# A two-layer decoder trunk on one core: the pair loop of TensorE on a fixed slot of the program, waits moved to their use, two k-tiles moved, two PSUM slots swapped

## The reference

```
h = rms_norm(x, norm_g);  z = h @ w_in      # columns of z feed all that follows
y_rnn = (rg_lru(x_rnn) * silu(g_rnn)) @ rg_out
y_sc  = (sc_b * conv3(sc_c * x_sc) * silu(g_sc)) @ sc_out
q = rms_norm(rms_norm(c_q) @ w_uq);  k = rms_norm([rms_norm(c_kv) @ w_uk, k_rope]);  v = rms_norm(c_kv) @ w_uv
y_att = (causal_attention(rope(q), rope(k), v) * silu(g_att)) @ mla_out     # 8 heads
x = x + (sig(g0) * y_rnn + sig(g1) * y_sc + sig(g2) * y_att) @ w_out
```

## Time and profile before

| | before |
|---|---|
| median of 3 runs | 1804.34 us (1803.9 to 1805.08) |
| profiled execution: own time / span | 1801.34 / 1799.5 us |
| mean granted clock of TensorE | 0.991 |
| busy: PE, PEld | 1742.7 us (97%), 1634.6 us (91%) |
| busy: POOL, DVE, ACT | 1184.6 us (66%), 807.1 us (45%), 469.6 us (26%) |
| chain that ended last | PE 95% |

### The profile page before, as it was taken

How to read it: one execution, slowest core, us unless ns; L and a number is a source line. 1 busy time by engine, 2 the same in 40 slices (tenths; PEclk the granted TensorE clock), 3 DMA queues, 4 the chain that set the end, 5 groups by cost and what they waited for, 6 DMA issues and landing times.

```text
span 1799.5 us, 32868 instructions
## 1 busy us (share of the span) xinstructions
PE 1742.7 (97%) x12264; PEld 1634.6 (91%) x12264; DVE 807.1 (45%) x1373; ACT 469.6 (26%) x843; POOL 1184.6 (66%) x1365
## 2 busy tenths in 40 slices
PE   3998998989999999999999999999999999999999
PEld 3998998989999999999999899999998888888887
DVE  3764554436464453212246645555556544522121
ACT  3422323222233223101124323232322333311110
POOL 6474644536677886777775747465557888877773
PEclk9999999999999999999999999999999999999999
DMA  3322221212222323222342212212122222332233
GB/s 126 136 71 65 71 81 43 93 54 71 83 83 93 105 82 119 93 94 83 122 152 74 93 64 70 80 64 80 54 86 91 91 93 93 105 128 95 94 118 107
DMA packets 47515, 162.03 MB, mean 90 GB/s; under 512 B 5408, under 2 KB 6816, under 8 KB 47136
## 3 DMA queue, kind: packets, MB, share of 16 engines
q1 hardware_dynamic: 41328, 146.56, 25.0%
q10 hardware_dynamic: 6112, 14.39, 2.2%
HBM read 152.27 MB, written 10.81 MB: 91 GB/s over the span
## 4 chain that ended last, share of the span: by engine, by line
PE 95%; issue 1%; POOL 1%; DVE 1%; ACT 1%; DMA 0%; ACTq 0%; POOLq 0%; DVEq 0%
PE slots L507 83%; PE slots L565 4%; PE slots L598 2%; PE slots L657 2%; PE slots L541 2%; PE slots L583 1%; POOL early L467 1%; DMA residual_or_merged<-xt 0%; DVE spare L1116 0%; ACT early L911 0%; PE slots L568 0%; DVE branch_lo L1107 0%; PE slots L550 0%; ACT x_square L810 0%; DVE early L1160 0%
## 5 line engine op out<-in xcount | busy, mean ns | idle before, releaser
L419 POOL TENSOR_TENSOR w_lo<-w_raw,w_hi 128x256 fp32r<-128x256 f32 x1004 | 828.4, 856 | 20.9
L414 POOL TENSOR_SCALAR w_hi<-w_raw 128x1024 fp32r<-128x1024 f32 x251 | 284.9, 1135 | 412.9 <-PE slots L507 404.1
L507 PE MATMUL slots<-h_hi,w_hi 128*128 128x264 f32 (+1 forms) x2112 | 523.0, 312 | 0.0
L507 PE MATMUL slots<-h_lo,w_hi 128*128 128x264 f32 (+1 forms) x2112 | 516.5, 309 | 0.0
L507 PE MATMUL slots<-h_hi,w_lo 128*128 128x264 f32 (+1 forms) x2112 | 516.2, 309 | 0.0
L507 PEld LDWEIGHTS slots<-h_hi,w_hi 128*128 128x128 f32 x2112 | 344.0, 189 | 19.1
L507 PEld LDWEIGHTS slots<-h_hi,w_lo 128*128 128x128 f32 x2112 | 343.1, 189 | 19.1
L507 PEld LDWEIGHTS slots<-h_lo,w_hi 128*128 128x128 f32 x2112 | 343.0, 189 | 17.6
L507 PE MATMUL slots<-branch_hi,w_hi 128*128 128x264 f32 (+1 forms) x576 | 143.6, 313 | 27.9 <-ACT causal_r L830 27.9
L507 PE MATMUL slots<-branch_lo,w_hi 128*128 128x264 f32 (+1 forms) x576 | 142.8, 311 | 0.0
L507 PE MATMUL slots<-branch_hi,w_lo 128*128 128x264 f32 (+1 forms) x576 | 142.4, 311 | 0.0
(11 more groups left out here) (241 smaller groups left out, 2867.1 us busy)
## 6 DMA issues: line engine op xcount, KB each, us to landing
w_raw<-w_units SPq DMA_DIRECT2D x251, 512.0 KB, 3.3
stream<-sc_acc ACTq DMA_DIRECT2D x16, 264.0 KB, 3.1
sc_back<-stream SPq DMA_DIRECT2D x2, 2112.0 KB, 9.6
x_old<-stream SPq DMA_DIRECT2D x16, 264.0 KB, 4.3
stream<-residual_or_merged ACTq DMA_DIRECT2D x16, 264.0 KB, 2.1
ab_raw<-w_units SPq DMA_DIRECT2D x8, 512.0 KB, 4.1
residual_or_merged<-xt ACTq DMA_DIRECT2D x4, 528.0 KB, 7.9
stream<-xt ACTq DMA_DIRECT2D x1, 2112.0 KB, 10.7
```

Source lines behind the costliest of these rows:

```text
L414: pool.tensor_scalar(hi, raw, 1.0, 1.0, ALU.mult, ALU.mult).then_inc(sem("hi_part"), 1)
L419: op = pool.tensor_tensor(lo[:, cols], raw[:, cols], hi[:, cols].bitcast(F32), ALU.subtract)
L507: mm = pe.matmul(out[:, a_, 0:t1 - t0], w(k), x(k)[:, t0:t1], start=(n == 0), stop=(n == 3 * ks - 1))
```

## The change

It has six parts.

1. The pair loop of TensorE is built by `nc.Fori` with `head_slot` 0: a marker ahead of the loop tells the loader to put the loop's first instruction on the first slot of a 16 KB piece of the program, and code ahead of it branches over the gap. This is done in both layers.
2. TensorE's three waits for constants are moved: `made` to the token sums of x, `params_in` and `consts_ready` to the rotation of the key in CQ, in the first layer only.
3. Two k-tiles of `c0` are issued ahead of the token sums of the queries in each pair, and 12 instead of 14 behind them (`FILLS`).
4. `spread_k0` and `spread_k1` change their PSUM slots: 0 and 1 instead of 1 and 0.
5. The squares of x go through four buffers instead of two (two tiles of `h_tile` are lent), with waits to match.
6. ACT squares a query latent ahead of copying it, and DVE adds the third square ahead of `q_lower(2)`; the addition now waits for the square by itself.

```diff
--- before.py
+++ after.py
@@ -71,7 +71,7 @@
 FILL = ("c0", "x0", "g0", "b0", "ga0", "c1", "x1", "g1", "b1", "ga1")
-FILLS = (14, 5, 5, 6, 6, 7, 2, 6, 6, 7, 7, 6)
+FILLS = (2, 12, 5, 5, 6, 6, 7, 2, 6, 6, 7, 7, 6)
 STAGES = {"NORM": (1, 0, 0), "CQ": (1, 6, 2), "ATT": (4, 12, 0), "RG": (4, 8, 0), "MR": (4, 4, 0),
           "MS": (4, 4, 0), "OUT": (2, 4, 0)}
 
@@ -84,7 +84,7 @@
            ("stat_kr", 2, "cq_mm"), ("rot", 3, "cq_mm"), ("stat_q", 1, "cq_mm")],
     "ATT": [("va", 2, "att_mm"), ("kn0", 0, "att_mm"), ("kn1", 1, "att_mm"), ("vb", 3, "unit_used"),
             ("qn0", 0, "att_mm"), ("stat_k", 1, "att_mm"), ("qn1", 2, "unit_used"), ("qr", 3, "att_mm"),
-            ("spread_k0", 1, "att_mm"), ("spread_k1", 0, "att_mm"), ("rot", 3, "att_mm"), ("stat_q", 2, "att_mm"),
+            ("spread_k0", 0, "att_mm"), ("spread_k1", 1, "att_mm"), ("rot", 3, "att_mm"), ("stat_q", 2, "att_mm"),
...
@@ -257,6 +257,7 @@
                 x_sq = [sb(f"x_square{n}", [P, T], F32, norm) for n in range(2)]
                 n_diag = sb("norm_diag", [P, T], F32, norm)
                 h_tile = [sb(f"h_tile{n}", [P, T], F32, norm) for n in range(3)]
+            x_sq += h_tile[0:2]
             y2_hi, y2_lo = sb("rnn_hi", [P, KT, T], F32R, mix), sb("rnn_lo", [P, KT, T], F32R, mix)
             with ExitStack() as gt:
                 sb("gate_hole", [P, 54592 // 4], F32, gt)
@@ -601,9 +602,6 @@
                                            start=(j == 0 and n == 0), stop=(j == last and n == 2))
                 mm.then_inc(sem("att_mm"), 1)
 
-            pe.wait_ge(sem("made"), 5)
-            pe.wait_ge(sem("params_in"), 48)
-            pe.wait_ge(sem("consts_ready"), 2)
             for l in range(DEPTH):
...
@@ -614,6 +612,8 @@
 
                 latent("kv0", 0)
                 latent("kv1", 1)
+                if l == 0:
+                    pe.wait_ge(sem("made"), 5)
                 out = free("NORM", l, 0, "stat")
                 pe.wait_ge(*at("x_summed", l, 0, KT - 1))
                 token_sums(out, [spare[0]]).then_inc(sem("norm_mm"), 1)
@@ -632,6 +632,9 @@
                 token_sums(out, [kr_sq[0:ROPE]]).then_inc(sem("cq_mm"), 1)
 
                 out = free("CQ", l, 0, "rot")
+                if l == 0:
+                    pe.wait_ge(sem("params_in"), 48)
+                    pe.wait_ge(sem("consts_ready"), 2)
                 for a_ in range(2):
                     mm = pe.matmul(out[:, a_, 0:HALF], rotate, gatt[1][:, a_ * HALF:(a_ + 1) * HALF],
                                    start=True, stop=True)
@@ -639,7 +642,7 @@
                 out = free("CQ", l, 0, "stat_q")
                 pe.wait_ge(*at("q_lat_summed", l, 0, 2))
                 token_sums(out, [q_lat_sq[0]]).then_inc(sem("cq_mm"), 1)
-                with pe.Fori(0, PAIRS) as p:
+                with nc.Fori(0, PAIRS, engines=bass.OrderedEngineSet([pe.engine]), head_slot={pe.engine: 0}) as p:
 
                     pe.wait_ge(*at("kv_lo", l, 0, KV))
 
@@ -715,6 +718,7 @@
                             if k == KT - 1:
                                 mm.then_inc(sem("unit_used"), 1)
 
+                    fill(FILLS[0])
                     stat = free("ATT", l, p, "stat_q")
                     pe.wait_ge(*at("q_summed", l, p, 2))
                     for k, which in enumerate((slice(0, 4), slice(4, 7), slice(7, 10))):
@@ -722,7 +726,7 @@
                         if k == 2:
                             mm.then_inc(sem("att_mm"), 1)
                         fill(1)
-                    fill(FILLS[0])
+                    fill(FILLS[1])
...
@@ -731,11 +735,11 @@
                     pe.wait_ge(*was_read("ATT", l, p, "rot"))
                     for n in range(10):
                         scores(l, p, n // 5, n % 5)
-                        fill(FILLS[n + 1])
+                        fill(FILLS[n + 2])
                         if n == 5:
                             attend(l, p, 0)
                         turn(l, p, n // 5, n % 5)
-                    fill(FILLS[11])
+                    fill(FILLS[12])
                     attend(l, p, 1)
                     assert filled[0] == len(FILL) * KT
 
@@ -805,9 +809,9 @@
 
             def x_square(l, c):
 
-                if c >= 2:
-                    act.wait_ge(*at("x_summed", l, 0, c - 1))
-                act.activation(x_sq[c % 2][:], xm[:, c, :], ACT.Square).then_inc(sem("x_squared"), 1)
+                if c >= 4:
+                    act.wait_ge(*at("x_summed", l, 0, max(1, c - 4)))
+                act.activation(x_sq[c % 4][:], xm[:, c, :], ACT.Square).then_inc(sem("x_squared"), 1)
 
...
@@ -841,9 +845,9 @@
                 def q_latent(n):
                     act.wait_ge(*ready("CQ", l, 0, f"q{n}"))
                     src = slot(slot_of("CQ", f"q{n}"))
+                    act.activation(halves(q_lat_sq[n][:]), src, ACT.Square).then_inc(sem("lat_squared"), 1)
                     act.activation(halves(cq_hi[:, n, :]), src, ACT.Identity, bias=zero,
                                    scale=hparam(l, CQ_G + n)).then_inc(sem("cq_hi"), 1)
-                    act.activation(halves(q_lat_sq[n][:]), src, ACT.Square).then_inc(sem("lat_squared"), 1)
 
                 def h_upper(k):
                     act.wait_ge(*at("h_full", l, 0, k + 1))
@@ -1113,7 +1117,7 @@
                 dve.wait_ge(*at("x_squared", l, 0, c + 1))
                 if c > 1:
                     dve.wait_ge(*at("x_summed", l, 0, c - 1))
-                dve.tensor_tensor(spare[0][:], x_sq[0][:] if c == 1 else spare[0][:], x_sq[c % 2][:],
+                dve.tensor_tensor(spare[0][:], x_sq[0][:] if c == 1 else spare[0][:], x_sq[c % 4][:],
                                   ALU.add).then_inc(sem("x_summed"), 1)
 
             dve.memset(token[:, 15:16], 0.0).then_inc(sem("x_ready"), KT)
@@ -1155,6 +1159,7 @@
                                              ALU.subtract).then_inc(freed("CQ", f"q{n}"), 1)
 
                 def add_q_square(n):
+                    dve.wait_ge(*at("lat_squared", l, 0, KV + n + 1))
                     if n > 1:
                         dve.wait_ge(*at("q_lat_summed", l, 0, n - 1))
                     dve.tensor_tensor(q_lat_sq[0][:], q_lat_sq[0][:], q_lat_sq[n][:], ALU.add).then_inc(
@@ -1210,8 +1215,8 @@
                 for n in range(KV):
                     dve.wait_ge(*at("kv_hi", l, 0, n + 1))
                     lo_part(kv_lo[:, n, :], kv_gained[n][:], kv_hi[:, n, :], "kv_lo")
+                add_q_square(2)
                 q_lower(2)
-                add_q_square(2)
 
                 dve.wait_ge(*ready("CQ", l, 0, "stat_kr"))
                 dve.wait_ge(*at("rinv_sq", l, 0, 1))
```

## The result

| | before | changed |
|---|---|---|
| median (range, runs) | 1804.12 us (1802.23 to 1805.08, 4) | 1751.72 us (1750.27 to 1752.76, 4) |
| profiled execution: own time / span | 1801.34 / 1799.5 us | 1751.97 / 1750.2 us |
| mean granted clock of TensorE | 0.991 | 0.999 |
| busy: PE, POOL, DVE, ACT | 97, 66, 45, 26% | 99, 68, 46, 27% |

The changed kernel takes 0.971 of the time, 95% interval 0.9693 to 0.9727: 52.4 us less in the medians, 49.3 less between the two profiled spans. The forecast was 1753.7 us, 50.6 less.

What follows compares the result with a forecast made beforehand. TensorE, busy 97% of the span, was taken as the bound, so only its waits and low clock could be won: 17.1 + 2.3 + 6.5 + 15.8 + 6.6 + 2.3 = 50.6 us, from 1804.3 to 1753.7, range 1747 to 1766.

Steps and rivals of the forecast that it cites:

- start: Kernel start: first matmul no longer waits for constants, sums of x begin at 24.9 instead of 42.04; 17.1 us.
- latent sums: Latent sums, twice: squaring before copying and adding before the split removes TensorE's wait for DVE's addition; 2.3 us.
- query sums: Query sums, eight times: two k-tiles in front shrink the 0.91 us wait for POOL to 0.10; 6.5 us.
- back-edge: Layer 0's loop branch, three times: the aligned loop stays loaded, so stalls of 5.12, 5.30 and 5.34 go; 15.8 us.
- cold behind it: After layer 0's three back-edge stalls: 24 matmuls at 1.2 GHz no longer take 5.11 us against 2.89; 6.6 us.
- clock elsewhere: Two other slow-clock stretches behind removed waits, first pair and near 1094 us: half of 4.9 won, 2.3 us.
- Rival 3: Start: stop and go behind DVE keeps TensorE at 1.2 GHz through kv1, sums at 28.8; 1758 us, chance 0.10.
- 70.5 to 71.5: Latent sums: when DVE's addition would run, with the square made first and the addition in front of the split.
- I take it that eight fit: Layer 0's loop: seven 16 KB program pieces touched and one fetched ahead all stay loaded; 15.8 us rests on it.
- Rival 1: Loop's back-edge: the head is still fetched each time, stall about 2.1 us; gain 41, time 1763, chance 0.10.
- Rival 2: Loop head: the alignment does nothing, nine pieces still touched, 22.4 us stay; gain 28.2, time 1776, chance 0.04.
- Rival 4: Loop entered by a jump: pieces not fetched ahead, 1.8 us per crossing, 79 us lost; time 1855, chance 0.02.

Runs made afterwards that it cites:

- add_between: Changed kernel with DVE's addition of the third square between the two splits of the key-value latent instead of behind both; 1754.46 us.
- no_swap: Changed kernel with the key spreads back in their old slots, the two k-tiles staying in front of the query sums; 1761.3 us.
- slot_128: Changed kernel with the pair loop's first instruction on slot 128 of a piece instead of slot 0; 1752.82 us.
- slot_144: Changed kernel with the pair loop's first instruction on slot 144 of a piece instead of slot 0; 1763.09 us.
- plain_loop: Changed kernel with the pair loop built plainly, without the fixed slot for its head; 1774.79 us.
- three_waits: Changed kernel, third square's addition between key-value splits, token sums of x behind q0's second k-tile, key-value norm diagonal before h's sixth tile; 1755.1 us.
- only_fill: Kernel before with only the two k-tiles in front of the query sums and the swapped spread slots; 1793.84 us.
- no_front_fill: Changed kernel with all 14 k-tiles behind the query sums again, none in front, swapped slots kept; 1768.49 us.
- only_slot: Kernel before with only the fixed slot for the pair loop's head, in both layers; 1785.05 us.

## Why the prediction was right, step by step

The forecast (1753.7) was 2.0 us above the median. The terms, forecast against measured between the two profiles:

| term | forecast | measured |
|---|---|---|
| start | 17.1 | 17.0 (42.04 to 25.08) |
| latent sums | 2.3 | 1.3 |
| query sums | 6.5 | 6.0 (8 x 0.75) |
| back-edge | 15.8 | 15.8 |
| cold behind it | 6.6 | 6.6 |
| clock elsewhere | 2.3 | 3.1 |
| new wait for `norm_diag` (0.55), less the 0.10 idle in that place before | 0 | -0.45 |
| sum | 50.6 | 49.3 (spans: 49.3) |

**Start.** Right to 0.1 us, by its steps too. TensorE's wait for unit 1 (0.68) and for the last addition (0.65) are the two that the working had in it. The price of the two edits was tested apart: 10.4 us up to the loop for the waits alone with four buffers, and 7.3 in the medians for the four buffers, of which about half is clock. Rival 3 falls: TensorE was through with kv1 0.65 us ahead of the sums and waited for DVE. In the three executions with the longer wait for unit 1 (last section) the clock did fall once more near 20 us, and in two of them the sums began at 26.7 and 26.9. "Behind this point everything keeps its distances" was off by 0.45 us: DVE's diagonal for the key-value norm is late by that much.

**Latent sums.** The mechanism held (layer 0 waits for nothing), the size didn't. The step that failed is "70.5 to 71.5" for both layers: it took DVE to be free when the square is ready. In layer 1 DVE was still in its two splits, stretched by POOL, and 0.97 of 1.15 us stayed. add_between showed that moving the addition alone wins nothing there.

**Query sums.** Right. No wait of 0.1 for DVE's spread shows in the list. no_swap confirms the bound from below: the forecast had TensorE stand 1.44 us for slot 0 without the swap, and it is 1.42 to 1.43 in each of eight pairs.

**Back-edge.** The choice between seven and nine, "I take it that eight fit", was right, and slot_128 and slot_144 now show it. Rival 1's price was worked out at 2.1 us; where slot_144 brings that case about it is 2.05 to 2.25. Rival 2 is what plain_loop shows, 1774.79 against 1776. Rival 4 falls: in the changed kernel no piece is waited for within a pair. Its mechanism does show once, in slot_144, where the piece behind the head comes 0.72 us late after the loop is entered. The restart: behind the stalls of 5.1 to 5.3 us in before and plain_loop the next 24 matmuls take 5.1 to 5.5 us, and 4.45 behind the one of 4.69; a stall of 2.2 us left them at 3.1 in one case of three (slot_144, the second) and at 4.6 in two.

**Clock elsewhere.** Right in size by luck: the profiles show 1.5 won in the first pair of layer 0, 3.1 won at 1098 us, 1.5 lost at 936. Its count of the evidence was wrong too: the earlier trace rows has ten waits of this kind (eight for POOL, two for DVE), and with two dips behind them eight kept the clock, not six. What the term missed is that a profile of one execution is a poor witness of it. Twelve profiled kernels have a wait of 0.97 to 1.15 us for the latent addition in layer 1, right ahead of the loop (all but add_between and three_waits). The clock fell behind it in eight and stayed in four (before, plain_loop, slot_128, only_fill). The clock goes with the spread of a few microseconds between executions: no_swap took 1760.75 us at 1.000 and 1765.86 at 0.997. The gain in medians (52.4) is above the 49.3 between the profiles since the profiled execution of before, 1801.34, lies 2.8 us under its median, and that of the changed kernel, 1751.97, 0.3 over.

## What to carry to other kernels

Count the instructions of a hot loop in pieces of the program (256 here) from the slot of its head: with seven touched the loop ran without a fetch, with eight every piece came anew in each round and the head was waited for, and the distance between the two was 16 slots. A wait of under a microsecond on the bounding engine can cost 3 us more when its clock falls behind it (no_front_fill, only_slot), so price it at itself and at itself plus a dip, and take several executions before believing either. Before reordering a helper engine's work, follow every slot that its later reads still hold.

## What the runs showed of the hardware that was not expected

- The fetch runs ahead by a whole piece even when only nine instructions of the last piece are used: slot_144 fetches nine packets in a pair.
- A short wait and a fall of the clock don't go together firmly. Behind eight waits of 1.4 us (no_swap) no pair's clock fell; behind eight of 0.9 it fell in one (before), two (no_front_fill) or three (only_slot). What sets it stays open.
- Where steps of DVE and POOL meet, the one that begins first keeps its time and the other is stretched, so that a shift of 0.1 us decides who pays: 1.80 against 1.01 us for the same five diagonals, 2.15 against 1.32 for the same two splits, as in all 24 cases above.
- The start varies from one execution to the next: TensorE stood in front of unit 1 for 0.7 us in seven of the ten profiles that have this wait and for 1.9 in three (no_front_fill, no_swap, three_waits), where POOL's first split began at 6.15 to 6.38 us; where it was 0.7 it began between 5.57 and 6.13. In the first two of the three the loop was reached 1.7 and 1.8 us later than in the changed kernel.
